# Two-block fp32 transformer stack on one core: wide products that end half by half, two weights split earlier, identity products at four turns and before the experts

## The reference, cut to what matters

```python
# first block
h = rmsnorm(x, norm1_g);  parts = split_columns(h @ w_in)
ya = moba_attention(...);  yb = nsa_attention(...)
merged = g[:, :, 0] * (ya @ w_up_a) + g[:, :, 1] * (yb @ w_up_b)
x = x + merged @ w_out                                    # wide product "out"
x = x + peer_ffn(rmsnorm(x, norm2_g), peer_wq, k1, k2, peer_u, peer_v)
# second block, i = 0, 1
x = x + attention(rmsnorm(x)) @ w_o      # i = 0, "wo";  i = 1: pooling instead
x = x + cross_attention(rmsnorm(x), rmsnorm(mem)) @ xattn_w_o[i]   # "xo0", "xo1"
x = x + conv_gated_ffn(rmsnorm(x), w_up, conv_w, conv_b, w_down)   # "ffd0", "ffd1"
return rmsnorm(x, final_norm)
```

## Time and profile before

| | |
|---|---|
| median of 3 runs | 1855.48 us (1854.06 to 1856.56) |
| profiled execution | 1856.75 us, span 1855.0 us |
| busy share | TensorE 96%, weight load 86%, VectorE 60%, ScalarE 51%, GpSimd 39% |
| chain that ended last | TensorE 72%, VectorE 17%, "issue" 6%, ScalarE 4%, GpSimd 1% |
| mean granted clock of TensorE | 0.986 |
| DMA | 313.67 MB, mean 169 GB/s |

### The profile page before, as it was taken

One profiled execution on the slowest core, in us unless ns is written; L12 is line 12 of the kernel. 1 busy time (PEld: TensorE's weight loads), 2 busy tenths in 40 slices (PEclk: granted clock), 3 DMA queues, 4 the chain that ended last, 5 costly groups with the idle time before them and its releaser, 6 DMA issues.

```text
span 1855.0 us, 32146 instructions
## 1 busy us (share of the span) xinstructions
PE 1786.3 (96%) x11558; PEld 1595.5 (86%) x11558; DVE 1120.1 (60%) x2239; ACT 946.0 (51%) x1533; POOL 728.0 (39%) x338
## 2 busy tenths in 40 slices
PE   8998989999999999999999999988999999999998
PEld 6995789889789999999999998866899978889986
DVE  6647648789764444444444444865459964449982
ACT  5567455458544444444444444666465544545543
POOL 0250266459244444444444443002244443234443
PEclk9998899999999999999999999999999999999999
DMA  7660354611455555555556665733455554535552
GB/s 292 211 217 5 125 173 147 217 39 51 148 192 195 189 182 181 188 190 187 181 181 231 235 212 178 243 118 125 142 187 178 182 185 145 171 120 178 181 183 78
DMA packets 84717, 313.67 MB, mean 169 GB/s; under 512 B 9360, under 2 KB 9488, under 8 KB 83216
## 3 DMA queue, kind: packets, MB, share of 16 engines
q1 hardware_dynamic: 82912, 304.44, 48.8%
q10 hardware_dynamic: 1712, 7.97, 1.2%
HBM read 304.77 MB, written 7.60 MB: 168 GB/s over the span
## 4 chain that ended last, share of the span: by engine, by line
PE 72%; DVE 17%; issue 6%; ACT 4%; POOL 1%; DVEq 0%; ACTq 0%; POOLq 0%; PEldq 0%
PE bank L768 67%; DVE cv L2252 4%; DVE cv L2242 4%; DVE wsplit L1717 3%; PE bank L1122 3%; DVE ff L1735 1%; POOL wsplit L1263 1%; DVE ff L1734 1%; ACT probs L1427 1%; PE bank L948 1%; ACT projq L1427 1%; PE bank L806 1%; ACT H L1353 0%; DVE X L1776 0%; DVE uptmp L2005 0%
## 5 line engine op out<-in xcount | busy, mean ns | idle before, releaser
L768 PEld LDWEIGHTS bank<-HT,wsplit 128*128 128x128 f32 x5952 | 732.7, 192 | 13.1 <-issue 2.8
L768 PE MATMUL bank<-HT,wsplit 128*128 128x256 f32 x5952 | 737.8, 284 | 1.1 <-DVE HT L1751 0.8
L1294 POOL TENSOR_TENSOR wsplit<-raw,wsplit 128x1024 fp32r<-128x1024 f32 x111 | 291.2, 2624 | 377.7 <-ACT wsplit L1587 377.7
L768 PE MATMUL bank<-wsplit,wexp 128*128 128x512 f32 x1536 | 375.9, 395 | 2.0 <-DVE wexp L2158 2.0
L1587 ACT ACTIVATE wsplit<-raw 128x1024 fp32r<-128x1024 f32 x238 | 251.3, 1058 | 184.3 <-PE bank L768 177.1
L768 PEld LDWEIGHTS bank<-wsplit,wexp 128*128 128x128 f32 x1536 | 279.7, 188 | 62.2 <-issue 2.4
L2138 DVE TENSOR_TENSOR wsplit<-raw,wsplit 128x1024 fp32r<-128x1024 f32 x127 | 167.9, 1322 | 224.8 <-ACT wsplit L1587 224.8
L1263 POOL TENSOR_TENSOR wsplit<-raw,wsplit 128x1024 fp32r<-128x1024 f32 x70 | 170.8, 2441 | 333.1 <-ACT wsplit L1333 333.0
L1263 POOL TENSOR_TENSOR wsplit<-raw1b,wsplit 128x1024 fp32r<-128x1024 f32 x45 | 109.2, 2426 | 314.8 <-ACT wsplit L1333 314.8
L1333 ACT ACTIVATE wsplit<-raw 128x1024 fp32r<-128x1024 f32 x148 | 155.5, 1058 | 110.5 <-PE bank L768 103.1
L1717 DVE TENSOR_TENSOR wsplit<-raw,wsplit 128x1024 fp32r<-128x1024 f32 x78 | 102.8, 1322 | 105.9 <-ACT wsplit L1333 105.3
(11 more groups left out here) (264 smaller groups left out, 2117.5 us busy)
## 6 DMA issues: line engine op xcount, KB each, us to landing
raw<-weights SPq DMA_DIRECT2D x148, 512.0 KB, 4.0
raw<-expert_v SPq DMA_DIRECT2D x127, 512.0 KB, 3.5
raw<-expert_u SPq DMA_DIRECT2D x119, 512.0 KB, 4.4
raw1b<-weights SPq DMA_DIRECT2D x102, 512.0 KB, 4.0
raw1a<-weights SPq DMA_DIRECT2D x48, 512.0 KB, 4.3
early_u<-expert_u SPq DMA_DIRECT2D x5, 512.0 KB, 3.4
raw1a<-expert_u SPq DMA_DIRECT2D x4, 512.0 KB, 4.3
parked<-memT SPq DMA_DIRECT2D x1, 2048.0 KB, 7.3
```

The costliest lines, as they stand in the source:

```text
L768: ins = pe.matmul(out, lhsT, rhs, start=start, stop=stop, **kw)
L1294: pool.tensor_tensor(wsplit[:, s, 1, :], raw0[:, s, :], f32(wsplit[:, s, 0, :]), ALU.subtract).then_inc(u_lo, 1)
```

## The change

Three edits. The first signals a wide product by halves: wide_done counts 4 for each product instead of 2, all readers wait for their half, and the order of the last products changes.

```diff
-        def wait_wide_done(eng, name, t):
-            eng.wait_ge(wide_done, T * WIDE.index(name) + t + 1)
+        def wait_wide_done(eng, name, t, h):
+            eng.wait_ge(wide_done, 4 * WIDE.index(name) + 2 * t + h + 1)
...
-                products(kt - 1, last, 0).then_inc(wide_done, 1)
-                products(kt - 2, w, 1)
-                state["frees"] = frees
-                products(kt - 1, last, 1).then_inc(wide_done, 1)
+                for h in range(2):
+                    products(kt - 1, last, 0, h).then_inc(wide_done, 1)
+                for h in range(2):
+                    products(kt - 2, w, 1, h)
+                    if h == 1:
+                        state["frees"] = frees
+                    products(kt - 1, last, 1, h).then_inc(wide_done, 1)
...
                 for t in range(T):
-                    wait_wide_done(dve, name, t)
                     for h in range(2):
+                        wait_wide_done(dve, name, t, h)
                         o = dst[:, t, h * 512:(h + 1) * 512]
                         dve.tensor_tensor(o, o, PS[2 * t + h][:, :], ALU.add).then_inc(wide_out, 1)
```

The second edit adds identity products, which write a part of a bank that is overwritten later:

```diff
+            def keep_busy(b, n):
+                for _ in range(n):
+                    pe.matmul(b[:, 0:P], ident, smalls[:, 0:P], start=True, stop=True)
...
-            def turn(name, H):
+            def turn(name, H, b=None, fill=(0, 0, 0)):
                 for t in range(T):
+                    keep_busy(b, fill[t])
                     pe.wait_ge(norm_h, T * NORMS.index("mem" if name[:3] == "mem" else name) + t + 1)
...
+                keep_busy(b, fill[T])
...
+            turn("norm1", H1, PS[7], (5, 2, 0))
+            turn("norm2", Hp, open_bank(("pq", 0)), (7, 3, 2))
+                    turn("x0", H2, open_bank(("xq", 0, 0)), (7, 3, 2))
+                    turn("ffn1", H2, open_bank(("ffu", 1, 0)), (7, 3, 2))
...
+            keep_busy(PS[2], 7)
             wait_freed(pe, ("ua", EARLY - 1))
             pe.sem_inc(a_v, BEGIN)
```

The third edit is on ScalarE at the end of the feed-forward loop:

```diff
                         full(("ffu", i, f))
+                        if f == NF - 1:
+                            split_to(UNIT["ffd", i, 0] + 4)
                         if f >= 2:
                             act.wait_ge(conv_m, NF * i + f - 1)
...
                     if f:
+                        if f == NF:
+                            split_to(UNIT["ffd", i, 0] + 5)
                         act.wait_ge(conv_d, NF * i + f)
```

More of the change, by code:

```diff
@@ L479, in wait_expert_slot @@
             else:
-                wait_wide_done(eng, "peer", T - 1)
+                wait_wide_done(eng, "peer", T - 1, 1)
         def v_turn(e):
@@ L851, in wide, with products @@
                     wait_wide(pe, WIDE[WIDE.index(name) - 1])
[L852 to L856, removed]
+                def products(k, w, t, h):
+                    return mm3(PS[2 * t + h][:, :], lambda a: src[:, a, k, tok(t)],
+                               lambda b: w(b)[:, h * 512:(h + 1) * 512], k == 0, k == kt - 1)
                 for k in range(kt - 2):
@@ L1152, in times_v @@
                                   lambda b: wsplit[:, 2 + s, b, h * 512:(h + 1) * 512], start, stop, skip_group_check=True)
-                ins.then_inc(wide_done if stop else a_v, 1)
+                        if stop:
+                            ins.then_inc(wide_done, 1)
+                if not stop:
+                    ins.then_inc(a_v, 1)
+            keep_busy(PS[2], 7)
             wait_freed(pe, ("ua", EARLY - 1))
@@ L1235, in _ @@
                     mem_key(3, 0)
-                turn(f"x{i}", H2)
+                if i:
+                    turn("x1", H2)
+                else:
+                    turn("x0", H2, open_bank(("xq", 0, 0)), (7, 3, 2))
                 if i:
@@ L1248, in _ @@
                     mem_key(1, 0)
-                turn(f"ffn{i}", H2)
+                if i:
+                    turn("ffn1", H2, open_bank(("ffu", 1, 0)), (7, 3, 2))
+                else:
+                    turn("ffn0", H2)
                 if i == 0:
@@ L1531, in _ @@
             for t in range(T):
-                wait_wide_done(act, "xv0", t)
                 for h in range(2):
+                    wait_wide_done(act, "xv0", t, h)
                     act.activation(Hp[:, t, h * 512:(h + 1) * 512], PS[2 * t + h][:, :], ACT.Copy).then_inc(wide_out, 1)
@@ L1638, in _ @@
             for t in range(T):
-                wait_wide_done(act, "xv1", t)
                 for h in range(2):
+                    wait_wide_done(act, "xv1", t, h)
                     act.activation(H2[:, t, h * 512:(h + 1) * 512], PS[2 * t + h][:, :], ACT.Copy).then_inc(wide_out, 1)
@@ L2180, in _ @@
             for t in range(T):
-                wait_wide_done(dve, "peer", t)
                 for h in range(2):
+                    wait_wide_done(dve, "peer", t, h)
                     o = X2[:, t, h * 512:(h + 1) * 512]
```

16 lines of the change are left out of this document (7 added, 9 removed).

## The result

The changed kernel takes 1846.41 us (median of 5, 1845.09 to 1849.88), against 1855.48 us before on the same chip. The ratio is 0.9953, with a 95% interval of 0.9941 to 0.9964. On a second chip it was 1847.05 us against 1855.92 us, ratio 0.9962 (0.9947 to 0.9977). The forecast was 1847.2 us. The profiled execution took 1845.26 us (span 1843.5), 11.49 us less than that of before; the medians lie 9.07 us apart.

What follows compares the result with a forecast made beforehand. TensorE, busy 96% of the span, was taken as the bound, so gains lay in its waits and low clock. Gains 3.03 + 6.95 + 0.2 less costs 0.64 net 9.54 us, from 1856.75 to 1847.2 us; range 1842.0 to 1853.0.

Steps and rivals of the forecast that it cites:

- Halves: Six joints of wide products outside norm2, x0 and ffn1: signalling each half shortens the add chain, gaining 3.03 us in all.
- peer to attn: Joint with memory-key products in its gap: bounds 0 and 0.65 us, gain taken as 0.3 us.
- Bare turns: norm2, x0 and ffn1: identity products keep the clock at 2.4 GHz; gains 2.8, 2.8 and 1.35 us, sum 6.95 us.
- The likeliest case: Whole kernel: the forecast itself, with the clock kept at norm2, x0 and ffn1; 1845.5 to 1849.5 us, 45% chance.
- the clock falls anyway: Rival at norm2, x0 and ffn1: clock still drops, costing 5.0 of 6.95 us, so 1852.2 us; 24% chance.
- other products in the gap: TensorE's gaps at turns: claimed that other products there made the difference to whether the clock stayed at 1.00.
- The cost at norm1: First turn: two identity products delay the second block, 0.44 us lost; bounds -0.4 (gain, by an earlier clock rise) and +0.9.
- my own sign: First layer's first product: starting 0.44 us later confirms the cost of identity products at norm1; starting earlier refutes it.
- The other 0.2 us, before the experts: Seven identity products before the experts' second products delay TensorE's signal to VectorE: cost 0.2 us, bounds 0 and 0.8.
- Down products: Feed-forward joints: early splits turn TensorE waits of 1.64 and 0.80 us into 0.7 and 1.7; 0.1 us gained each.
- The rival without the hold: Feed-forward joints: GpSimd's subtraction does not hold up VectorE, both stalls go, 4.7 us more gained, 1842.5 us; 13% chance.
- The slower rival: Self attention, 1244 to 1265 us: shifted idleness brings 1.2 GHz, costing 8.5 to 14.8 us, 1855.7 to 1862.0 us; 6% chance.

Runs made afterwards that it cites:

- c2_transposes: The changed kernel with each identity product replaced by two transposes of the same tile: 1847.12 us, ratio 0.9951.
- a2_fills: The kernel before with only the identity products added, at norm1, norm2, x0, ffn1 and the experts: 1849.35 us, ratio 0.9973.
- a4_vector_late: The changed kernel with VectorE instead of GpSimd making the odd units' lower parts in the second feed-forward down product, unit 3's early: 1844.74 us, ratio 0.995.
- b1_vector_both: The changed kernel with VectorE instead of GpSimd making the odd units' lower parts in both feed-forward down products: 1841.78 us, ratio 0.9924.
- a5_attn_fills: The changed kernel with identity products added in the attention parts too: 1860.55 us, ratio 1.0026.

## Why the prediction was right, point by point

**Halves.** Right, by its own steps: 0.58 to 0.61 at out, wo, xo1, ffd0 and ffd1, 0.49 and 0.48 at xv0 and xv1, 0.42 at ffn0, the same to 0.02 us in two traces and with the halves alone. One term was mis-sized: peer to attn gave 0.68 and not 0.3. I took the middle of the bounds of 0 and 0.65 because memory-key products stand in that gap; the whole add left the chain.

**Bare turns.** The likeliest case came, and by its mechanism. All three turns are at 1.00 in the 12 traces with identity products or transposes there, 36 turns of 36; in the traces without them five of six fell (three of three before, two of three with the halves alone). The clock alone gave 1.90, 1.77 and 0.58 us, 4.25 us where 5.0 was forecast. The rival "the clock falls anyway", with the rule on transposes behind it, is refuted by these turns and by c2_transposes. Two steps of mine were wrong without harm. An identity product is two PE instructions, 0.23 us and not 0.11, because I halved the 0.22 us of a row that counts instructions; the seven fill 1.72 of the gap of 1.6 to 1.8 us, with nothing to spare. And "other products in the gap" is not the whole cause: x0 kept its clock with the halves alone, and three products do as well as seven.

**norm1 and the experts.** The cost at norm1 is real and was mis-sized, and something else varies more. Two products cost 0.85 us there and not 0.44 (a2_fills), the doubled price again, and the early rise of the clock that I had named as the other bound took it back in the trace of the comparison (clock up at 8.36 us, +0.06), but not in the second (9.95 us, -0.53). By my own sign the first trace refutes the cost and the second confirms it; one trace was too few for that sign. The other 0.2 us, before the experts, did not come. The -0.32 in the table is no such cost: the first second product still starts with the lead unchanged at 6.68 us, and the lead changes only between 532 and 555 us, which I cannot explain. VectorE's first weighting still starts after 0.85 us of idleness, as in the earlier trace rows, released by TensorE's own signal:

```profile
472.17 1.72 PE L802 MATMUL bank<-smalls 128*128 128x128 f32 x14
...
472.98 0.43 DVE L2176 TENSOR_TENSOR act_e<-early_a,gates 128x256 f32<-128x256 f32 x1 [0.85 <-PEq L1169]
```

It starts at 472.98, before the identity products end at 473.89, and 0.23 us after ScalarE's copy, as in the kernel before. In this trace the signal that stands behind the products in TensorE's program is recorded at 472.8: it did not wait for them. I had named the wait and assumed that the signal comes after the products. What I had not counted is a fall of the clock in this bare wait, 1.57 us in one trace of the three without products there.

**Down products.** Right to 0.1 us in each wait. The changed kernel's first joint, where the earlier trace rows was before: VectorE, GpSimd and TensorE:

```profile
1486.91 2.39 DVE L1756 CAST ff<-cv 128x256 fp32r<-128x256 f32 x1
...
1484.17 4.98 POOL L1281 TENSOR_TENSOR wsplit<-raw,wsplit 128x1024 fp32r<-128x1024 f32 x2 [3.51 <-ACT wsplit L1351]
...
1491.04 5.83 PE L768 MATMUL bank<-wsplit,ff 128*128 128x512 f32 x24 [0.80 <-DVE wsplit L1739]
1498.49 3.73 PE L768 MATMUL bank<-wsplit,ff 128*128 128x512 f32 x15 [1.61 <-DVE wsplit L1739]
```

Unit 3 follows unit 1 at once on GpSimd (two subtractions in 4.98 us, to 1489.15), the cast that was 0.29 us takes 2.39, and 1.64 and 0.80 us have become 0.80 and 1.61 (forecast 0.7 and 1.7). The rival without the hold is refuted, and a4_vector_late and b1_vector_both take the 2.8 us a joint that the early splits did not get. By the Trainium skill (SBUF — State Buffer, section "SBUF: two separate sides") the port pair that VectorE and GpSimd share is held for the whole instruction; a cast that ends at 1489.30, right behind GpSimd's subtraction, agrees.

**The slower rival.** Its mechanism came in small: the clock was low in the self attention from 1230.3 to 1233.7 and from 1254.2 to 1257.6 us, and 1.30 us was lost there. In all it was low there for 6.8 us, as in the trace of before, but at other places. The loss was not more, and the first attention gave 3.66 us of the same kind. I had treated these stretches as fixed. They differ in each execution, so one trace against another is uncertain by some 4 us.

**The sum.** The terms were right: 9.54 us forecast, 9.12 measured in the trace, 9.07 between the medians. The profiled difference of 11.49 us holds 2.36 us of luck. So does a little of the closeness of 1847.2 to 1846.41: I took the terms off the profiled 1856.75 us, 1.27 us above the median; from the median of 1855.48 us they give 1845.9 us, as near on the other side.

## What to carry to other kernels

In a gap of 2 us a busy TensorE can lose its clock, and it works at half the rate for 3 to 7 us behind it. A few products or transposes of 128 columns in such a gap kept the clock in every trace here, and where they fitted into the gap they cost nothing. Put them only where the engine idles, count their instructions in a trace first, and not among products of few rows and columns, where they cost 13 us here. Where a trace begins, compare the rate of the products with the clock that the view prints. If a weight is split earlier on a second engine, ask what that engine's longer instruction holds up. Here the early split alone gave 0.03 us a joint; with the work moved to the engine that had been held up it was 2.8 us.

## What the hardware showed that I had not expected

- In a5_attn_fills TensorE was 100% busy by the profile from 140 to 158 us, first in products of 64 rows by 15 columns with one full product behind each four, and its clock was at 0.50 for 13.7 us of it. Busy is not enough.
- A plain float32 product of 128 by 128 is two PE instructions (14 for seven), a float32 transpose is one (16 for 16), at the same 0.115 us each.
- At the start of the execution TensorE works at half of the later rate (0.21 us for a transpose against 0.11) until a moment between 8.4 and 16.7 us, which differs in each trace. The clock records begin at that moment; before it the view prints 1.00 for want of a record.
- The same program falls to the low clock at different places in different executions: 33 to 52 us in all for the kernel before, with 0.36 us more time for each.
- A signal that stood alone in TensorE's program behind 14 instructions was recorded at 472.8 us, 1.1 us before the last of them ended.
